# Three expert tiles instead of two finished by one-hot products, in a mixed SGU/pooling and grouped-MoE block

## The reference, cut to what matters

```python
def grouped_moe(h, router_w, router_bias, w_gate, w_up, w_down):
    ...
    g = jnp.einsum('td,edf->tef', t, w_gate)
    u = jnp.einsum('td,edf->tef', t, w_up)
    a = jax.nn.silu(g) * u * combine[:, :, None]
    y = jnp.einsum('tef,efd->td', a, w_down)
    return y.reshape(B, S, D)

def reference(...):
    ...
        x = x + g_f[:, None, :] * grouped_moe(hf, router_w, router_bias,
                                              w_exp_gate[l], w_exp_up[l], w_exp_down[l])
    return rmsnorm(x, final_norm_g)
```

## Time and profile before

| | us |
|---|---|
| median of 3 runs | 801.79 |
| the profiled execution, its own time | 800.28 |
| its span, first to last instruction | 798.5 |
| TensorE busy (share of the span) | 732.5 (92%) |
| VectorE busy | 588.3 (74%) |
| ScalarE busy | 389.9 (49%) |
| GpSimd busy | 192.0 (24%) |
| mean granted TensorE clock, as a share of full speed | 0.956 |

### The profile page before, as it was taken

One profiled execution on the slowest core, in us unless ns is written; L12 is line 12 of the kernel. 1 busy time (PEld: TensorE's weight loads), 2 busy tenths in 40 slices (PEclk: granted clock), 3 DMA queues, 4 the chain that ended last, 5 costly groups with the idle time before them and its releaser, 6 DMA issues. The chain is left out here.

```text
span 798.5 us, 10609 instructions
## 1 busy us (share of the span) xinstructions
PE 732.5 (92%) x3354; PEld 603.7 (76%) x3355; DVE 588.3 (74%) x785; ACT 389.9 (49%) x352; POOL 192.0 (24%) x79
## 2 busy tenths in 40 slices
PE   2589999999999999999999389999999999999990
PEld 2468888866888888886788278888888888888880
DVE  3772334765475766768464898999999999999955
ACT  6542523343323141315134357777777777777723
POOL 1000001301000000000052101455555554445532
PEclk9789999999999999999997589999999999999996
DMA  8797330331365563827463528699999999999685
GB/s 316 266 367 242 105 131 23 136 105 53 108 210 183 173 221 127 293 71 257 174 236 124 200 66 320 230 357 413 350 363 373 359 368 381 361 395 372 244 164 162
DMA packets 105651, 187.66 MB, mean 235 GB/s; under 512 B 6991, under 2 KB 50063, under 8 KB 105628
## 3 DMA queue, kind: packets, MB, share of 16 engines
q1 hardware_dynamic: 98076, 173.58, 60.2%
q0 software_dynamic: 5936, 12.14, 5.5%
q10 hardware_dynamic: 1616, 1.65, 0.6%
HBM read 180.47 MB, written 16.25 MB: 246 GB/s over the span
## 5 line engine op out<-in xcount | busy, mean ns | idle before, releaser
L776 DVE TENSOR_TENSOR wsplit<-raw,wsplit 128x2048 fp32r<-128x2048 f32 x132 | 299.2, 2287 | 79.8 <-ACT wsplit L526 52.9
L705 ACT ACTIVATE wsplit<-raw 128x2048 fp32r<-128x2048 f32 x96 | 184.1, 1920 | 73.3 <-PE ps L1369 73.3
L474 POOL DMA_INDIRECT expert_rows<-work,dest_now x15 | 107.8, 7186 | 113.8 <-DVE work L1260 104.9
L1367 PE MATMUL ps<-wsplit,hgT 128*128 128x512 f32 x280 | 112.5, 402 | 5.0 <-DVE hgT L1179 5.0
L1369 PE MATMUL ps<-wsplit,hgT 128*128 128x512 f32 x280 | 110.6, 395 | 0.0
L1368 PE MATMUL ps<-wsplit,hgT 128*128 128x512 f32 x280 | 110.5, 395 | 0.0
L1367 PE MATMUL ps<-hT,wsplit 128*128 128x512 f32 x256 | 101.0, 395 | 1.0 <-DVE mx L934 1.0
L1368 PE MATMUL ps<-hT,wsplit 128*128 128x512 f32 x256 | 99.6, 389 | 0.0
L1369 PE MATMUL ps<-hT,wsplit 128*128 128x512 f32 x256 | 99.6, 389 | 0.0
L833 DVE SCALAR_TENSOR_TENSOR raw<-raw,c_silu 128x256 f32 (+1 forms) x128 | 62.0, 485 | 13.3 <-DMA raw<-in_w_ada 9.3
L1367 PEld LDWEIGHTS ps<-wsplit,hgT 128*128 128x128 f32 x280 | 53.4, 191 | 16.4 <-DVE hgT L1179 5.7
(11 more groups left out here) (256 smaller groups left out, 1187.0 us busy)
## 6 DMA issues: line engine op xcount, KB each, us to landing
raw<-in_w_exp_gate SPq DMA_DIRECT2D x32, 1024.0 KB
raw<-in_w_exp_up SPq DMA_DIRECT2D x32, 1024.0 KB
raw<-in_w_exp_down SPq DMA_DIRECT2D x32, 1024.0 KB
raw<-in_w_ada SPq DMA_DIRECT2D x24, 1024.0 KB
raw<-in_w_in SPq DMA_DIRECT2D x20, 1024.0 KB
expert_rows<-tmp SPq DMA_DIRECT2D x4, 1024.0 KB, 13.0
raw<-in_w_branch_a SPq DMA_DIRECT2D x4, 1024.0 KB
raw<-in_w_branch_b SPq DMA_DIRECT2D x4, 1024.0 KB
```

Source lines behind the costliest of these rows:

```text
L474: g.indirect_dma_start(out=y_dram, out_offset=bass.IndirectOffsetOnAxis(ap=dest_now[:, 0:1], axis=0), in_=y, in_offset=None, bounds_check= ...
L705: A_(wsplit[:, c, 0, :], raw[:, c, :], ACT.Copy).then_inc(hi_ready, 1)
L776: V.tensor_tensor(wsplit[:, n, 1, :], raw[:, slot, :], wsplit[:, n, 0, :].bitcast(F32), ALU.subtract).then_inc(lo_ready, 1)
L1367: nc.tensor.matmul(out, w_hi, m_hi_, start=first, stop=False)
```

## The change

Three expert tiles, `tiles-3` to `tiles-1`, go through one-hot products. GpSimd's loop ends one turn earlier, the last gather follows it alone, and the accumulating transfers wait for `tiles - 3` scatters. The result of tile `tiles-3` stays in `y` and is split there. The one-hot products are ordered by token tile, and VectorE sums, roots and scales token tiles 0 and 1 ahead of 2 and 3; it now scales 0, 1 and 3, and GpSimd and ScalarE share only token tile 2. The last roots use PSUM for their intermediates, and ScalarE forms the factor -0.5*(mean + EPS) (`fin_half`). `gfin` moves into `hg` and is loaded once the last gather has landed.

```diff
-FIN_X = (4, 5, 6, 8)
+TAIL = 3
+FIN_X = (2, 4, 6, 8)
...
-        gfin = work[:, 4 * D:5 * D]
+        gfin = hg
+        y_hi = [wsplit[:, 2 + j // 2, 0, j % 2 * D:(j % 2 + 1) * D] for j in range(TAIL)]
+        y_lo = [wsplit[:, 2 + j // 2, 1, j % 2 * D:(j % 2 + 1) * D] for j in range(TAIL)]
...
         # SyncE
+            wait_reg(sp, gathered, tiles * 16 + 16)
             sp.dma_start(gfin, A["final_norm_g"].partition_broadcast(P)).then_inc(gfin_in, 16)
-            for t in (1, 3):
-                sp.wait_ge(fin_ready, t // 2 + 1)
+            for i, t in enumerate((0, 1, 3)):
+                sp.wait_ge(fin_ready, i + 1)
                 sp.dma_start(out_rows[:, t, :], x_tiles[:, t, :]).then_inc(out_done, 16)
...
         # GpSimd
-            with pool.Fori(2, tiles - 1) as i:
+            with pool.Fori(2, tiles - 2) as i:
                 gather(i + 2)
                 scatter(i - 1)
+            gather(tiles)
             wait_reg(pool, gathered, tiles * 16 + 16)
-            wait_reg(pool, scattered, tiles * 16 - 32)
+            wait_reg(pool, scattered, tiles * 16 - 48)
...
-            for t in (0, 2):
-                pool.wait_ge(fin_x, FIN_X[t])
-                g.tensor_tensor(scaled[:, t // 2, :], x_tiles[:, t, :], gfin, ALU.mult).then_inc(fin_gain, 1)
+            pool.wait_ge(fin_x, FIN_X[2])
+            g.tensor_tensor(scaled, x_tiles[:, 2, :], gfin, ALU.mult).then_inc(fin_gain, 1)
...
         # ScalarE
+            act.wait_ge(y_ready, tiles - 2)
+            act.wait_ge(chunk_used, tiles * 6 + 28)
+            A_(y_hi[0], y, ACT.Copy).then_inc(tail_hi, 1)
             root_table(2)
             act.wait_ge(y_ready, tiles - 1)
-            act.wait_ge(chunk_used, tiles * 6 + 28)
-            A_(y_hi[0].rearrange("p (b n) -> p b n", b=2), ps[:, 5:7, :], ACT.Copy).then_inc(tail_hi, 1)
+            A_(y_hi[1].rearrange("p (b n) -> p b n", b=2), ps[:, 5:7, :], ACT.Copy).then_inc(tail_hi, 1)
...
                     A_(root[:, t - 1:t + 1], stats[:, 27 + t:29 + t], ACT.Sqrt, bias=eps_col[:, 0:1],
                        scale=1.0 / D).then_inc(rooted, 1)
+                    A_(fin_half[:, t - 1:t + 1], stats[:, 27 + t:29 + t], ACT.Identity, bias=half_eps[:, 0:1],
+                       scale=-0.5 / D).then_inc(rooted, 1)
...
         # VectorE
-            for j in range(2):
+            for j in range(TAIL):
                 for t in range(NT):
                     ins = V.tensor_scalar(tail_sel[:, j, t * P:(t + 1) * P], iota1[:, :], float(t * P - 1),
                                           tail_tok[:, j:j + 1], ALU.add, ALU.is_equal)
...
+            dve.wait_ge(tail_hi, 1)
+            V.tensor_tensor(y_lo[0], y, y_hi[0].bitcast(F32), ALU.subtract).then_inc(tail_lo, 1)
             dve.wait_ge(chunk_used, tiles * 6 + 30)
...
             def final_root(col, count):
 
-                m, half, z = stats[:, col:col + 2], nrm[:, 0:2], nrm[:, NT:NT + 2]
-                dve.wait_ge(rooted, NT + 1 + count)
+                m, half = stats[:, col:col + 2], fin_half[:, col - 28:col - 26]
+                z, z2, q = ps[:, 0, 0:2], nrm[:, col - 28:col - 26], ps[:, 0, 4:6]
+                dve.wait_ge(rooted, NT + 2 * count)
                 step(V.reciprocal(z, root[:, col - 28:col - 26]))
-                step(V.tensor_scalar(half, m, -0.5 / D, -0.5 * EPS, ALU.mult, ALU.add))
+                step(V.reciprocal(z2, root[:, col - 28:col - 26]))
                 done()
-                step(V.tensor_tensor(m, z, z, ALU.mult))
+                step(V.tensor_tensor(q, z, z2, ALU.mult))
                 done()
-                step(V.tensor_tensor(m, m, half, ALU.mult))
+                dve.wait_ge(rooted, NT + 1 + 2 * count)
+                step(V.tensor_tensor(q, q, half, ALU.mult))
                 done()
-                V.scalar_tensor_tensor(out=m, in0=m, scalar=1.5, in1=z, op0=ALU.add,
+                V.scalar_tensor_tensor(out=m, in0=q, scalar=1.5, in1=z2, op0=ALU.add,
                                        op1=ALU.mult).then_inc(fin_rms_ready, 1)
                 dve.wait_ge(fin_rms_ready, count)
...
-            dve.wait_ge(gfin_in, 16)
-            for t in (1, 3):
-                final_root(27 + t, t // 2 + 1)
+            def final_scale(t):
                 V.scalar_tensor_tensor(out=x_tiles[:, t, :], in0=x_tiles[:, t, :], scalar=stats[:, 28 + t:29 + t],
                                        in1=gfin, op0=ALU.mult, op1=ALU.mult).then_inc(fin_ready, 1)
+
+            for t in range(2):
+                for half in range(2):
+                    final_sum(t, half, 2 * t + half + 1)
+            dve.wait_ge(gfin_in, 16)
+            final_root(28, 1)
+            final_scale(0)
+            for half in range(2):
+                final_sum(2, half, 5 + half)
+            final_scale(1)
+            for half in range(2):
+                final_sum(3, half, 7 + half)
+            final_root(30, 2)
+            final_scale(3)
...
         # TensorE
-            pe.wait_ge(tail_lo, 1)
+            pe.wait_ge(tail_lo, 2)
             pe.wait_ge(idx_ready, tiles + 1)
-            for half in range(2):
-                for t in range(NT - 1):
-                    tail_add(0, t, half, True, False)
-                    pe.wait_ge(tail_lo, half + 2)
-                    tail_add(1, t, half, False, True).then_inc(tail_mm, 1)
-            for half in range(2):
-                tail_add(0, NT - 1, half, True, False)
-                tail_add(1, NT - 1, half, False, True).then_inc(tail_mm, 1)
+            for t in range(2):
+                for half in range(2):
+                    for j in range(2):
+                        tail_add(j, t, half, j == 0, False)
+            for t in range(2):
+                for half in range(2):
+                    pe.wait_ge(tail_lo, half + 3)
+                    tail_add(2, t, half, False, True).then_inc(tail_mm, 1)
+            for t in range(2, NT):
+                for half in range(2):
+                    for j in range(TAIL):
+                        mm = tail_add(j, t, half, j == 0, j == TAIL - 1)
+                    mm.then_inc(tail_mm, 1)
```

More of the change, by code:

```diff
@@ L88, in tokens_moe_kernel @@
         aT_last = hgT[:, :, 0:NF, :]
-        with nc.sbuf_tensor("below_tail", [P, 3 * D], F32), nc.sbuf_tensor("tail_sel", [P, 2, SEQ], F32R) as tail_sel:
+        with nc.sbuf_tensor("below_tail", [P, 3 * D], F32), nc.sbuf_tensor("tail_sel", [P, TAIL, SEQ], F32R) as tail_sel:
             pass
@@ L109, in tokens_moe_kernel @@
         eps_col = sb("eps_col", [P, 1])
+        half_eps = sb("half_eps", [P, 1])
+        fin_half = sb("fin_half", [P, NT])
         root = sb("root", [P, NT + 3])
@@ L122, in tokens_moe_kernel @@
         dest_now = sb("dest_now", [P, 1], I32)
-        tail_idx = sb("tail_idx", [P, 2], I32)
-        tail_tok = sb("tail_tok", [P, 2])
+        tail_idx = sb("tail_idx", [P, TAIL], I32)
+        tail_tok = sb("tail_tok", [P, TAIL])
         iota_i = sb("iota_i", [P, P], I32)
@@ L148, in tokens_moe_kernel @@
         rt = work[:, 3 * D + NT * P:5 * D]
-        gfin = work[:, 4 * D:5 * D]
-        y_hi = [wsplit[:, 2 + j, 0, 0:D] for j in range(2)]
-        y_lo = [wsplit[:, 2 + j, 1, 0:D] for j in range(2)]
+        gfin = hg
+        y_hi = [wsplit[:, 2 + j // 2, 0, j % 2 * D:(j % 2 + 1) * D] for j in range(TAIL)]
+        y_lo = [wsplit[:, 2 + j // 2, 1, j % 2 * D:(j % 2 + 1) * D] for j in range(TAIL)]
         pair = [ps[:, 0:2, :], ps[:, 4:6, :], ps[:, 6:8, :], ps[:, 2:4, :]]
-        scaled = raw[:, 2:4, D:2 * D]
+        scaled = raw[:, 2, D:2 * D]
         rows_in = sem("rows_in")
@@ L428, in _ @@
             g.memset(eps_col[:, :], EPS)
+            g.memset(half_eps[:, :], -0.5 * EPS)
             g.memset(beats[:, :, :], 1.0)
@@ L734, in _ @@
             A_(aT_last[:, 0, :, :].rearrange("p k m -> p (k m)"), ps[:, 4, :], ACT.Copy).then_inc(aT_hi, 1)
+            act.wait_ge(y_ready, tiles - 2)
+            act.wait_ge(chunk_used, tiles * 6 + 28)
+            A_(y_hi[0], y, ACT.Copy).then_inc(tail_hi, 1)
             root_table(2)
             act.wait_ge(y_ready, tiles - 1)
-            act.wait_ge(chunk_used, tiles * 6 + 28)
-            A_(y_hi[0].rearrange("p (b n) -> p b n", b=2), ps[:, 5:7, :], ACT.Copy).then_inc(tail_hi, 1)
+            A_(y_hi[1].rearrange("p (b n) -> p b n", b=2), ps[:, 5:7, :], ACT.Copy).then_inc(tail_hi, 1)
             for half in range(2):
                 act.wait_ge(y_ready, tiles + half)
-                A_(y_hi[1][:, half * 512:half * 512 + 512], ps[:, LAST_BANK + half, :], ACT.Copy).then_inc(tail_hi, 1)
+                A_(y_hi[2][:, half * 512:half * 512 + 512], ps[:, LAST_BANK + half, :], ACT.Copy).then_inc(tail_hi, 1)
             for t in range(NT):
@@ L751, in _ @@
                        scale=1.0 / D).then_inc(rooted, 1)
[L752 to L758, removed]
+                    A_(fin_half[:, t - 1:t + 1], stats[:, 27 + t:29 + t], ACT.Identity, bias=half_eps[:, 0:1],
```

(25 more changed lines are left out.)

## The result

The changed kernel took a median of 795.98 us in 5 runs (795.6 to 798.49), the kernel before 801.79 in 5 (799.44 to 802.66). The ratio is 0.9938, with a 95% interval of 0.9918 to 0.9958, so 3.4 to 6.6 us shorter. The span of the profiled execution went from 798.5 to 794.0. The prediction was 798.0, range 796.8 to 800.7. The median lies 0.8 under the low end; the ratio, put on 801.79, gives 796.8, the low end itself. The span moved by -4.5, where -3.8 was forecast and the range stands for -5.0 to -1.1.

What follows compares the result with a forecast made beforehand. The start of the eight accumulating transfers was taken to set the end. Sums through last scaling gave -3.0 and stores -0.8, together -3.8 us: span 794.7, median 798.0, range 796.8 to 800.7.

Steps and rivals of the forecast that it cites:

- The start of the transfers: GpSimd's first accumulating transfer, released by the last gather, is issued at 754.3, 5.9 us earlier.
- the rival that took 135 throughout: Rival: accumulating transfers run at 135 GB/s throughout, tile 1 lands at 783.8, median 804.3; chance 0.05.
- TensorE becomes last for tiles 0 and 1: One-hot products of tiles 0 and 1 finish at 776.2 and 777.6, after their transfers at 773.5 and 775.9.
- Covered steps: Extra tail_sel writes, y_hi[0] and y_lo[0] ahead of the one-hot products hide in idle time: cost nothing.
- The finish: Sums, squares, roots and scalings to the end: last scaling starts at 788.9 against 791.91, -3.0 us.
- the surcharge of 0.1 for PSUM: Root steps up to the scaling: 0.1 us added to 0.84 for PSUM operands, bounds 0 and 0.3.
- The stores: SyncE's last store takes 4.1 us instead of 4.9: -0.8, bounds -1.4 and 0.
- The moved load of gfin: gfin's load, now beside the first accumulating transfers, costs them 1.3 us, or 2.5 at the slower rate.
- GpSimd's multiplication: GpSimd's one multiplication starts behind VectorE's scaling of tile 1 at 785.1 and ends at 787.5, before the last root.
- What removed the stall of 2.0: The small TENSOR_SCALAR's 2.0 us stall goes through the new split, one GpSimd multiplication; PSUM route worth about nothing.

Runs made afterwards that it cites:

- the runs with later transfers: Changed kernel with one or three small loads on GpSimd's queue ahead of the first accumulating transfer; one run each, end moved by 0.1 and 6.2 us.
- the kernel with GpSimd first: Changed kernel with three small PSUM copies on VectorE ahead of the scaling of tile 1; one run, last scaling moved by 2.4 us.
- SBUF roots: Changed kernel with the old final_root back in SBUF and ScalarE's Identity dropped; ratio 0.9952 to the kernel before.
- three tiles with the old split: Kernel before with three one-hot tiles and early transfers; products, sums, roots, GpSimd's two multiplications and stores as before; ratios 0.9941 and 0.9937.
- the rearranged kernel: Against three tiles with old finish: PSUM roots, first roots ahead of tile 3, tile 0 scaled on ScalarE and stored at once; ratio 0.9908 to the kernel before.

## Why the prediction was right, and where it was not

- **The start of the transfers.** Forecast 754.3 on a gather that lands at 753.8; it was 753.32 on a gather at 752.6. In the second trace of the changed kernel the first issue stands 6.4 ahead of the common point, as forecast (6.5). Off the path by 2.2 to 3.5 us, so without effect. The stream ran at 207 to 213 GB/s from 762 on, with TensorE 2.00 busy of 2.00, so the rival that took 135 throughout fell.
- **TensorE becomes last for tiles 0 and 1.** The prediction's main step, shown: the first sum at 776.24 (forecast 776.3) waits for TensorE, the products end at 783.0 as forecast, and the runs with later transfers put the point where transfers take over at a landing 16.6 behind the common point. (The working had the products end 3.6 later than before; against 771.93 + 7.71 = 779.6 it is 3.4, and nothing used it.)
- **Covered steps.** tail_sel and y_lo[0] cost nothing, as forecast: the products start at 771.96 against 771.93.
- **The finish.** Each step came a little sooner than forecast: the last scaling at 788.49 and not 788.9. Of these 0.4, 0.14 lie ahead of the first scaling (781.21 against 781.35), 0.13 in the four scalings and pairs of sums behind it (1.20 from start to start, not 1.25), 0.05 in the square and 0.09 in the second root: the surcharge of 0.1 for PSUM was not there (0.87 and 0.86 from reciprocal to scaling, against 0.84).
- **The stores.** From the start of the last scaling to the end it took 6.6 before and 5.5 after: -1.1, forecast -0.8. SyncE's last one landed in 3.8.
- **The moved load of gfin.** The term of 1.3 measured a few tenths at most. Nothing hung on it.
- **GpSimd's multiplication.** The order came out as forecast, VectorE first, by a lead of 0.23 (783.61 and 783.84) that was the same in both traces. The row begins at 783.84 and lasts 3.25, of which 2.3 are work (2.34 in the kernel with GpSimd first): the row of the blocked instruction runs from its issue, wait included. It ended at 787.1 (forecast 787.5).
- **What removed the stall of 2.0.** The prediction said that the new split of the work did, and not the route through PSUM. The second half holds (SBUF roots: 0.15). The first is too narrow: three tiles with the old split have no stall either. TensorE's products then pace the sums, so GpSimd starts on its multiplications while sums are still running and is through as the roots begin, with -0.1 to 0.2 us to spare; with the new split it ends 0.5 ahead of the last root (787.09 and 787.63).
- **What the prediction never asked** is what the new order costs. It followed the changed kernel's own sequence and found an end under the old one. But behind TensorE's last product at 783.0, VectorE is still busy with tile 2's sums and a scaling, and the second sum of tile 3 starts 24.5 behind the common point where the old order has it at 22.2. So by the traces three tiles with the old finish are worth 5.9, stall and all, and the new finish gives 1.4 of it back; the times don't show the 1.4, but they do show that the rearranged kernel beats the changed one.
- **The size in the times.** The trace moved by 4.5, the medians by 5.8 and, in the second group of runs, by 5.7 (801.21 to 795.55); the intervals hold 4.5. The rest would be upstream of the common point. An estimate of how far kernels differ there: median, less 1.8 (time over span), less the table's end puts the common point at 760.6 to 761.1 for the changed kernel, 761.2 to 762.3 for the one before, and up to 762.9 for another. Whether that is the kernels or the executions, no run here settles. So of the distance between the forecast and the time, 0.4 (finish) and 0.3 (stores) are accounted for, and the rest is open.

## What to carry to other kernels

When a wait is taken away, work out what ends last instead, and then arrange the rest backwards from there: whatever stands behind the new last event must be only what depends on it. A part of a change that helps with the old bound can cost with the new one, so cost each part with the others in place. Read traces of a kernel with upstream scatter from a common event, not from the start of the span.

## What the runs showed of the hardware

- A VectorE scaling with two SBUF inputs and a GpSimd multiplication exclude each other, whichever starts first: 3.25 instead of 2.34 on GpSimd, or 3.08 and 2.39 instead of 1.28 on VectorE. The stall looks like a slow instruction, with no idle time before it. The one-input TENSOR_SCALAR of two columns was shut out as well (2.12 and 2.19 us instead of 0.15), but the RECIPROCAL of two columns just before it was not (0.17 at 783.28 above, and at 787.04 in the kernel before, 0.1 and 0.2 into a multiplication of GpSimd), and sums with one PSUM input ran at 0.69 beside GpSimd. By the Trainium skill (SBUF — State Buffer, Who interferes with whom) the second to issue is blocked for the whole length of the first; the two orders of these runs agree with it.
- The four accumulating issues took 3.83 beside VectorE's writes of tail_sel and 3.72 beside a subtraction with two SBUF inputs, while the gather beside such a subtraction took 2.13 and not 1.00, as the one at 456.10 of the kernel before did, with no work of VectorE on two SBUF inputs beside it. A scatter took 7.66 beside three such subtractions, and 1.01 at 756.34 beside the writes of tail_sel, which have one input. So it is the indirect issues that stretch, and not beside every VectorE instruction.
- A load of 8 KB on GpSimd's queue, with the wait for it, cost 3.0 to 4.0 us.
